# Row-by-row sums of the late modulation on GpSimd, and an earlier place for the context's key products

## The reference

```python
mod_x = (jax.nn.silu(c) @ w_ada + b_ada)[:, None, :]          # 6 * D_MODEL columns
sh_a_x, sc_a_x, g_a_x, sh_f_x, sc_f_x, g_f_x = jnp.split(mod_x, 6, axis=-1)
p_x = modulate(rms_norm(x, norm_mix), sh_a_x, sc_a_x) @ w_in
...
qx, kx, vx = attn_heads(q_at_x, k_at_x, v_at_x, q_norm, k_norm)   # RMSNorm per head
qc, kc, vc = attn_heads(q_at_c, k_at_c, v_at_c, q_norm, k_norm)
qx, kx = rope_2d(qx, rope), rope_2d(kx, rope)
# 8 heads, 2 key heads; each query sees +-128 latent keys, all 256 context keys, and a sink
y_at_x = window_attention_latent(qx, kx, vx, kc, vc, attn_sink)
```

## Time and profile before

| | us |
|---|---|
| median of 3 runs | 2536.14 (2535.06 to 2537.48) |
| the profiled execution | 2534.82 |
| its span | 2532.9 |
| TensorE busy | 2433.4 (96%) |
| VectorE busy | 1448.1 (57%) |
| GpSimd busy | 877.6 (35%) |
| ScalarE busy | 823.1 (32%) |
| projections of the attention, from about 59 | to 228.5 |
| windowed attention | 228.5 to about 432 |

### The profile page before, as it was taken

How to read it: one execution, slowest core, us unless ns; L and a number is a source line. 1 busy time by engine, 2 the same in 40 slices (tenths; PEclk the granted TensorE clock), 3 DMA queues, 4 the chain that set the end, 5 groups by cost and what they waited for, 6 DMA issues and landing times. The chain is left out here.

```text
span 2532.9 us, 40503 instructions
## 1 busy us (share of the span) xinstructions
PE 2433.4 (96%) x16150; PEld 2055.7 (81%) x16150; DVE 1448.1 (57%) x2281; ACT 823.1 (32%) x1900; POOL 877.6 (35%) x640
## 2 busy tenths in 40 slices
PE   5999999999999999999999999999899999999999
PEld 4778998888788888888888877878688888887887
DVE  6994674222666666666666663357755555564332
ACT  4223663200455464545546452101211111111100
POOL 1643765322514232241423222336333333332121
PEclk9999999999999999999999999999999999999999
DMA  7321332322001010000101003224311111114442
GB/s 270 93 75 55 121 126 84 100 75 84 20 16 35 10 43 26 18 26 18 35 10 35 26 18 107 88 94 143 138 50 50 46 46 50 50 37 126 124 136 91
DMA packets 52648, 177.02 MB, mean 70 GB/s; under 512 B 5360, under 2 KB 14960, under 8 KB 51184
## 3 DMA queue, kind: packets, MB, share of 16 engines
q1 hardware_dynamic: 50160, 170.24, 20.8%
q10 hardware_dynamic: 2304, 4.20, 0.4%
HBM read 148.20 MB, written 20.97 MB: 67 GB/s over the span
## 5 line engine op out<-in xcount | busy, mean ns | idle before, releaser
L205 PE MATMUL late_ps<-h_hi,late_w_hi 128*128 128x512 f32 x784 | 307.6, 392 | 6.1 <-ACTq L127 3.4
L206 PE MATMUL late_ps<-h_lo,late_w_hi 128*128 128x512 f32 x784 | 306.6, 391 | 0.0
L207 PE MATMUL late_ps<-h_hi,late_w_lo 128*128 128x512 f32 x784 | 306.6, 391 | 0.0
L188 POOL CAST late_w_hi<-late_w_raw 128x1024 fp32r<-128x1024 f32 x76 | 80.0, 1052 | 505.1 <-issue 378.0
L1515 PE MATMUL late_ps<-h_hi,dn_w_hi 128*128 128x512 f32 (+1 forms) x640 | 246.5, 385 | 0.0
L1515 PE MATMUL late_ps<-h_hi,dn_w_lo 128*128 128x512 f32 (+1 forms) x640 | 245.6, 384 | 0.0
L1515 PE MATMUL late_ps<-h_lo,dn_w_hi 128*128 128x512 f32 (+1 forms) x640 | 244.6, 382 | 0.0
L195 POOL TENSOR_TENSOR late_w_lo<-late_w_raw,late_w_hi 128x1024 fp32r<-128x1024 f32 x76 | 205.3, 2702 | 6.1
L2632 DVE SCALAR_TENSOR_TENSOR ffn_u<-ffn_pad,vectors,ffn_u 128x1024 f32<-128x1024 f32 (+1 forms) x90 | 198.1, 2201 | 3.2
L205 PEld LDWEIGHTS late_ps<-h_hi,late_w_hi 128*128 128x128 f32 x784 | 148.1, 189 | 37.8 <-issue 7.0
L207 PEld LDWEIGHTS late_ps<-h_hi,late_w_lo 128*128 128x128 f32 x784 | 148.2, 189 | 31.2
(11 more groups left out here) (400 smaller groups left out, 6297.2 us busy)
## 6 DMA issues: line engine op xcount, KB each, us to landing
late_w_raw<-in_w_up SPq DMA_DIRECT2D x44, 512.0 KB, 3.5
down_w_raw<-in_w_down SPq DMA_DIRECT2D x32, 704.0 KB, 4.3
late_w_ada<-in_w_ada SPq DMA_DIRECT2D x8, 2048.0 KB, 7.3
dn_w_raw<-in_w_dn SPq DMA_DIRECT2D x32, 512.0 KB, 3.8
w_ada<-in_w_ada SPq DMA_DIRECT2D x8, 1024.0 KB, 11.4
at_w_raw<-in_w_mg_at SPq DMA_DIRECT2D x16, 512.0 KB, 3.9
late_w_raw<-in_w_mg_dn SPq DMA_DIRECT2D x16, 512.0 KB, 3.7
late_w_raw<-in_w_out SPq DMA_DIRECT2D x16, 512.0 KB, 3.7
```

What stands on the lines that cost most here:

```text
L188: pool.tensor_copy(self.hi[j][:, :, :], self.raw[j][:, :, :]).then_inc(self.hi_made, 1)
L205: pe.matmul(out, self.hi[j][:, k, :], xh, start=(k == 0), stop=False)
L206: pe.matmul(out, self.hi[j][:, k, :], xl, start=False, stop=False)
L207: mm = pe.matmul(out, self.lo[j][:, k, :], xh, start=False, stop=(k == self.kt - 1))
```

## The change

In `attention_projections` the context's k products move ahead of the sums of squares of the last tile. In `window_attention` POOL makes the low part of each unit first, and behind it as many rows of the late modulation as keep 8 rows to 7 units: row 0 of a step is scaled straight into the sum, every other row is scaled in place and added to the sum. Each addition waits for its scaling (`ada_scaled`) and for the row before (`ada_summed`), row 0 from step 2 on for the columns of the step two before (`ada_used`), and each row for its half of the weights. The weights come in two loads of 1 MB, each issued when the four rows that it replaces are summed. The two gate tiles are split after units 14 and 24. TensorE's first column of a step waits for its last row.

```diff
@@ attention_projections, TensorE
+                def context_keys():
+
+                    raw_ready.wait(pe, NT - 1)
+                    pe.wait_ge(ctx_hi, KT)
+                    pe.wait_ge(ctx_lo, KT)
+                    for g in range(KV_HEADS):
+                        mm = w.product(pe, ps_main[0][:, g * CTX:(g + 1) * CTX], g, core.h_hi, core.h_lo, SEQ, CTX)
+                    mm.then_inc(kc_done, 1)
+
                 def tile(t, half, j):
...
                             if b == 1:
                                 mm.then_inc(w.used.sem, 1)
+                        elif b == 0:
+                            context_keys()
                         if b == 0:
                             sq_ready.wait(pe, t + 1)
...
                 std_ready.wait(pe, NT)
                 raw_ready.wait(pe, NT)
-                pe.wait_ge(ctx_hi, KT)
-                pe.wait_ge(ctx_lo, KT)
-                for g in range(KV_HEADS):
-                    mm = w.product(pe, ps_main[0][:, g * CTX:(g + 1) * CTX], g, core.h_hi, core.h_lo, SEQ, CTX)
-                mm.then_inc(kc_done, 1)
-
                 pe.wait_ge(ba_lo, 1)
@@ window_attention
+    HALF_K, SPLIT_AT = KT // 2, (10, 20)
...
-        ada_in, mod_made = core.sem("late_ada_in"), core.sem("late_mod_made")
+        ada_in, mod_made = [core.sem(f"late_ada_in{i}") for i in range(2)], core.sem("late_mod_made")
...
@@ window_attention, GpSimd
-                FIRST = 3
-                queries_low(AHEAD, FIRST)
-                for n in range(ADA_STEPS):
-                    u = AHEAD + n * XCH
-                    pool.wait_ge(ada_in, n * 16 + 16)
-                    pool.sem_inc(turns, 1)
-                    for k in range(KT):
-                        ins = pool.tensor_scalar(w_ada[:, k, :], w_ada[:, k, :], core.silu_c[:, k, 0:1], 1.0, ALU.mult,
-                                                 ALU.mult)
-                        if k == KT // 2 and n:
-                            queries_low(u, 1)
...
+                def ada_sum(n, k):
+
+                    pool.wait_ge(ada_in[k // HALF_K], n * 16 + 16)
+                    acc, c, w = ada_acc[:, n % 2, :], core.silu_c[:, k, 0:1], w_ada[:, k, :]
+                    if k == 0:
+                        if n >= 2:
+                            pool.wait_ge(ada_used, n - 1)
+                        ins = pool.tensor_scalar(acc, w, c, 1.0, ALU.mult, ALU.mult)
+                    else:
+                        pool.tensor_scalar(w, w, c, 1.0, ALU.mult, ALU.mult).then_inc(ada_scaled, 1)
+                        pool.wait_ge(ada_scaled, n * (KT - 1) + k)
+                        pool.wait_ge(ada_summed, n * KT + k)
+                        ins = pool.tensor_tensor(acc, acc, w, ALU.add)
+                    ins.then_inc(ada_summed, 1)
+
+                done = 0
+                for u in range(AHEAD, UNITS):
+                    queries_low(u, 1)
+                    while done < min(ADA_STEPS * KT, (u - AHEAD + 1) * KT // STEP_UNITS):
+                        ada_sum(*divmod(done, KT))
+                        done += 1
+                    if u - AHEAD in SPLIT_AT:
+                        at_w.split_tile(pool, SPLIT_AT.index(u - AHEAD), 0, SPLIT_AT.index(u - AHEAD), freed=False)
@@ window_attention, TensorE
-                            pe.wait_ge(ada_folded, n * 3 + 3)
+                            pe.wait_ge(ada_summed, (n + 1) * KT)
@@ window_attention, SP
-                    if n:
-                        sp.wait_ge(ada_folded, n * 3)
-                    sp.dma_start(w_ada[:, :, :], d["w_ada"][:, n + 2 * KT // SLOT_T]).then_inc(ada_in, 16)
+                    for i in range(2):
+                        ks = slice(i * HALF_K, (i + 1) * HALF_K)
+                        if n:
+                            sp.wait_ge(ada_summed, (n - 1) * KT + (i + 1) * HALF_K)
+                        sp.dma_start(w_ada[:, ks, :], d["w_ada"][:, n + 2 * KT // SLOT_T, ks]).then_inc(ada_in[i], 16)
```

More of the change, by code:

```diff
@@ L787, in window_attention @@
         pt_act, pt_dve, y_ready = Count(core, "pt_act"), Count(core, "pt_dve"), Count(core, "y_ready")
-        ada_scaled, ada_folded, ada_used = core.sem("late_ada_scaled"), core.sem("late_ada_folded"), core.sem("late_ada_used")
+        ada_scaled, ada_summed, ada_used = core.sem("late_ada_scaled"), core.sem("late_ada_summed"), core.sem("late_ada_used")
         y_stored = core.y_stored = [nc.alloc_semaphore(f"y_stored{j}") for j in range(2)]
@@ L811, in queries_low @@
                                            a.q_hi[:, u % AHEAD, :].bitcast(F32), ALU.subtract).then_inc(q_lo_made, 1)
-                FIRST = 3
-                queries_low(AHEAD, FIRST)
-                for n in range(ADA_STEPS):
-                    u = AHEAD + n * XCH
-                    pool.wait_ge(ada_in, n * 16 + 16)
-                    pool.sem_inc(turns, 1)
-                    for k in range(KT):
-                        ins = pool.tensor_scalar(w_ada[:, k, :], w_ada[:, k, :], core.silu_c[:, k, 0:1], 1.0, ALU.mult,
-                                                 ALU.mult)
-                        if k == KT // 2 and n:
-                            queries_low(u, 1)
-                    ins.then_inc(ada_scaled, 1)
-                    if n:
[L826 to L844, removed]
```

## The result

The changed kernel takes 2517.64 us (median of 4 runs, 2513.95 to 2523.01) against 2536.81 us (4 runs, 2535.06 to 2540.20), a ratio of 0.9922 with a 95% interval of 0.9902 to 0.9941. Timed again in other rounds it took 2518.05 us (6 runs) against 2535.47 (11 runs), a ratio of 0.9933 (0.9918 to 0.9947). The forecast was 2520.1 us, 16.0 us less than before, with a range of 2515.0 to 2526.5. The change is faster by 17 to 19 us.

What follows compares the result with a forecast made beforehand. TensorE, 96% busy, was taken as the bound, losing time in waits for Pool and at half clock. Part 1 (- 14.7 us) and part 2 (- 1.3) gave - 16.0 us: 2520.1 us from 2536.1, range 2515 to 2526.5.

Steps and rivals of the forecast that it cites:

- What bounds the kernel: TensorE, busy 96% of the span; in the attention stage ten waits for Pool cost it 13.4 us.
- Part 1: Attention stage, modulation sums row by row: 13.4 us of waits and 1.6 at half clock go, 0.3 come: 14.7 less.
- The half load: Landing time of a 1 MB load of modulation weights: 5.0 us, between 3.9 for 512 KB and 7.3 for 2 MB.
- The new wait: TensorE at unit 54 waits because step 7's load stands behind the store of y: 0.3 us, bounds 0 to 3.8.
- The room behind the second gate tile: Pool, unit 24's high part to unit 25's low part: 8.4 us of work, for which there are 10.2 us.
- The half clock: TensorE at 1.2 GHz from 415.70 to 419.10, behind the longest wait: cost 1.6 us, expected to go.
- Part 2: Projections, context's k products moved earlier into TensorE's wait for the squares: gain 1.27 us, bounds 0 and 2.5.
- The second gap: TensorE's 1.21 us wait for ScalarE's square root behind the sums of squares: stays, now ahead of the small projection.
- VectorE's cover: Last tile's reciprocal starts 2.9 us later, so its work ends about 196.6; 1 us left before the context's reciprocal.
- (a): Pool's waits within a row cost 0.25 us, not 0.08, giving 3 to 4 us of low-part waits: 2523.5 us, chance 0.14.
- (b): Half loads land late behind the store of y; steps 6 and 7 wait 1.0 and 3.8 us: 2524.6, chance 0.10.
- (c): Slower: Pool bounds the attention stage, with a row of 2.8 us and a step of 24.8 us: 2562 us, chance 0.06.

Runs made afterwards that it cites:

- x7_loads_first: Changed kernel with SP loading the modulation weights of step h + 2 ahead of the store of y, not behind it: 2518.80 us.
- x3_whole_loads: Changed kernel with one 2 MB load per step instead of two halves, Pool's order unchanged: 2559.33 us, ratio 1.0088 to the kernel before.
- x1: Kernel before with only the context's k products moved ahead of the last tile's sums of squares: ratio 0.9992 to the kernel before.
- x4_columns_later: Kernel before with TensorE's modulation columns one unit later (FIRST_COLUMN 11 instead of 10): 2532.37 us, ratio 0.9984.
- x5_row_long: Changed kernel with a second scaling by one, over 512 columns, in each of the 56 added rows: 2546.09 us, ratio 1.0038 to the kernel before.
- x2: Changed kernel with the context's products put back behind the wait for the last root: 2519.12 us, ratio 0.993 to the kernel before.
- x8: Changed kernel with loads ahead of the store of y and TensorE's wait for the last square root moved to the context's sums of squares: 2518.67 us.
- y1: Changed kernel, unaltered, timed again in other rounds: 2518.05 us against 2535.47 us for the kernel before.
- y2: Same kernel as x8, timed again beside the changed kernel: 2516.56 us against 2518.05 us.
- x9_rows_first: Changed kernel with Pool doing a unit's rows first and its low part behind them: 2521.38 us, ratio 0.9952 to the kernel before.
- x6_row_longer_a_bit: Changed kernel with a second scaling by one, over 128 columns, in each of the 56 added rows: 2529.10 us, ratio 0.9971 to the kernel before.

## Why the prediction was right, point by point

**What bounds the kernel.** Right. Ten waits for POOL of 11.8 us idle and their 0.16 us each, 13.4 us, went to 0.46. The reading by starts mattered: the idle column alone would have given 11.8.

**Part 1.** A row was put at 2.0 us, from 0.69, 1.27 and 0.08; the additions are 1.277 us and the gaps 0.08. The half load was put at 5.0 us between 3.9 and 7.3, and is 5.0. The new wait was put at unit 54 with 0.3 us, and is there with 0.26. A second one at unit 60, 0.20 us, I had not named: unit 60 follows the two rows that end step 7, and POOL was still behind from the late load. `x7_loads_first` shows that both come from the store ahead of the load. The stage was to lose 14.7 us and lost 14.85. That the 0.3 came so near is partly luck, since it was picked between bounds of 0 and 3.8 us. The room behind the second gate tile was counted too large: 8.4 us of work in 10.2 leave 1.8, and 0.75 us were left at unit 25.

By the figures of the Trainium skill ("DMA: Bandwidth & Descriptors", Anatomy of one DMA) a half would have been an estimated 4.4 us. Measured are 5.0, so they were low for the half as they were for the whole. The section gives them for DMAs that GpSimd issues, which the prediction passed over, and these loads are issued by SP. The eight more fixed costs didn't matter, since a half is issued four rows ahead; `x3_whole_loads` shows what it costs to save them.

**The half clock.** The forecast of 1.6 us held in the sum, but the cause is argued more than shown. In the kernels that waited 2 us or more for POOL in the stage's last ten units the clock was 0.50 at the end of that wait and behind it (the kernel before and the runs x1, x3, x4 and x5), and in those with no wait over 0.3 us it was 1.00 from there to the end of the stage (the changed kernel, x2, x7, x8, y1 and y2). But 2.02 us at 287.47 in the kernel before and 2.68 us at 379.38 in `x9_rows_first` have no such stretch behind them. No experiment took the wait away and left the rest; `x4_columns_later` was meant to, and its wait only moved.

**Part 2.** The path was to be 1.27 us shorter and is 1.48: the products take 5.75 us to the start of the sums (172.05 to 177.80) and not 5.86, and from there to L635 it is 3.08 us and not 3.19. The second gap stayed, where and as large as said (1.21 us). Mis-sized was VectorE's cover. I left it 1 us, with the tile's work ending at 196.6; it ends at 191.01, and 5.45 us are idle ahead of the context's reciprocal. The step that failed is "starts 2.9 us later, so ends 2.9 us later": its three products were slow before because POOL split the v weights beside them, and the split now comes earlier (below). Part 2 is read from traces alone: the timing doesn't separate the kernel without it (2519.12 us) from the changed one (2517.64 and 2518.05).

**The rivals.** (a) fell, the gaps are 0.08 us with two waits in a row. (b) was right about the place and not the size: 0.26 and not 3.8 us. (c) fell in the changed kernel, but its mechanism is real. Its point was wrong: I let a row last 2.57 us before the gain is eaten, and left out the 6.9 us of the gate tiles. The short extra scaling (a row of 2.0 + 0.39 us) took 10.8 us of the gain, the long one (2.7 us) all of it and more.

**What was not forecast.** 3 us more were gained between the first medians than the edited places explain. In the thirteen traces the stretch behind the stage lasts from 2102.3 to 2108.8 us with the same instructions, and the stretch to the last product of tile 9 from 172.05 to 176.99. Both are as wide apart among kernels that differ only in the stage as between before and after. So a profiled pair can gain or lose some us in places that nobody edited, and 16.3 us is what the change did to the two places that it edited.

Laid side by side matmul by matmul, the two traces show where the 3.5 us behind the stage arise. 1.5 us are the stretch at half clock at 647.8, which the kernel before has and the changed one hasn't. Another 2.3 us arise between 1730 and 1830 us, where TensorE waits for VectorE and the stretches at half clock fall at other instructions in each trace: a wait of 2.68 us (at 1793.32 before) is 0.58 us (at 1774.16) in the changed kernel. Ahead of tile 9 the kernel before has a stretch at half clock too (36.8) and the changed one none. The number of such stretches alone doesn't give the time: behind the stage they are 20.4 us before and 23.8 us after (the last 20 us left out), and 27.2 us in both `x3_whole_loads` and `x9_rows_first`, whose times there are 2103.2 and 2108.8 us. What sets where they fall is open.

## What to carry to other kernels

Where one engine feeds a saturated one and does background work besides, what counts is how much work and how many landings can stand between the moment when a feed could be made and when it is due: cut the work to grains that fit that slack, cut its loads into pieces that free their buffer early, and put the feed first. Then count the helper's whole work against the consumer's time, since past that margin each us of the helper is the consumer's. A wait removed at the consumer gains only what the next wait for the same producer leaves.

## What the runs showed of the hardware

**POOL and VectorE stop each other.** These are three rows of VectorE and POOL in the kernel before, where POOL splits the v weights (timeline, start us, duration):

```profile
184.86 2.40 POOL L195 TENSOR_TENSOR aproj_w_lo<-aproj_w_raw,aproj_w_hi 128x1024 fp32r<-128x1024 f32 x1
...
185.64 2.70 DVE L729 TENSOR_TENSOR qk_heads<-qk_turned,rope_tables 128x1024 f32<-128x1024 f32 x1
...
187.21 2.04 POOL L188 CAST aproj_w_hi<-aproj_w_raw 128x1024 fp32r<-128x1024 f32 x1
```

And the same product of VectorE after, with POOL's split over:

```profile
187.33 1.16 DVE L734 TENSOR_TENSOR qk_heads<-qk_turned,rope_tables 128x1024 f32<-128x1024 f32 x1
```

The product takes 1.16 us alone. Beside POOL it started at 185.64 and ended at 188.34, which is 1.08 us behind the end of POOL's subtraction (187.26). The cast, 1.03 us elsewhere, ended at 189.25, 0.91 behind the product. So each stood until the other was done, and nothing in these rows looks like sharing. The Trainium skill says so ("SBUF — State Buffer", SBUF: two separate sides): the port pair that the two share is an exclusive lock for the whole instruction, against a VectorE operation with two SBUF inputs, and the trace agrees. It also changes rival (c). The 3.37 us of L588 (177.96 to 181.33) that I took for a slow rate are a standing behind a product of VectorE that began just before it:

```profile
177.84 1.22 DVE L735 TENSOR_TENSOR qk_heads<-qk_heads,qk_rstd 128x1024 f32<-128x1024 f32 x1
```

This ends at 179.06, and L588 ends 2.27 us behind it. In the attention stage VectorE's large instructions read PSUM, and the 56 additions of the changed kernel lie between 1.266 and 1.293 us, so none of them shows such a standing.

**A stretch at half clock costs the stage little where another engine is the bound.** `x5_row_long` has 20.5 us at 0.50 within the stage and `x6_row_longer_a_bit` 6.8, yet the stage grew by 19.0 us where POOL's work grew by 18.0. The 1.4 us at the end of `x5_row_long` show the other side: there POOL's last low parts were made, and the stretch cost what it cost the kernel before, 1.6 us, within 0.2.
